# Five of the twelve products for xbc, in both layers of the first block, by seven part products instead of eight

## The chip, the cores and the metric

The kernel runs on one core of a Trainium2 chip, as one program and one launch. The metric is the device time in microseconds (us). The kernel before took 3345.99 us, the median of three runs that lay between 3344.57 and 3346.96 us. Everything is in 32-bit floats.

## What is computed

256 tokens of width 1024 go through a first block of two layers and then a second block of two layers. The change is in the layers of the first block. Cut to what matters, such a layer is:

```
h = h + 0.5 * swiglu(rms_norm(h), ffn1)
u = rms_norm(h, mix_norm)
(z_s, xbc, dt_s, qkv, z_d, b_d, a_d, gate_s, gate_d) = split(u @ w_in)
xbc = silu(causal_depthwise_conv(xbc, conv_w, conv_b))       # 4 taps, 3072 channels
y_s = state space branch of xbc, dt, z_s;  y_d = delta rule branch of qkv, z_d, b, a
h = h + (sigmoid(gate_s) * (y_s @ w_s) + sigmoid(gate_d) * (y_d @ w_d)) @ w_out
h = h + 0.5 * swiglu(rms_norm(h), ffn2)
```

The 3072 features of xbc come out of a matrix of 1024 x 3072, and the convolution along the tokens, one filter of four taps for each feature, is taken of them.

## The kernel before

Activations lie with features on the 128 partitions and tokens along the free dimension: `xT` holds the normed input as 8 tiles of 128 features x 256 tokens. The weights are read once, in order, as chunks of 1 MB (128 partitions x 2048 floats, 16 tiles of 128 x 128). SyncE issues one DMA for each chunk into a ring of three places; a place is written again when the first matmul of the chunk after it has run (`w_used`).

**A product.** A chunk of xbc gives 256 features (two tiles), and there are 12 chunks, so 12 products (named 0 to 11 below). `product` runs 16 matmuls with 256 tokens each, 8 for each of the two tiles, into one PSUM bank. Every matmul of 32-bit floats shows in the trace as two records. All matmuls of the large products have the line L331.

**By seven.** Other products of the kernel (`ffn1`, `z_d`, `gate_s` and others) take their chunk as a matrix of 2 x 2 quarters (half of the inputs, tile of the outputs), and the tokens as two halves of 128. The 2 x 2 by 2 x 2 product of quarters is then made with seven products of quarters in place of eight, at the price of sums: `tokens_by_dve` (L898 to L903) makes four sums of token quarters once for a stage, `weights_by_dve` (L885 to L890) four sums of weight quarters for every chunk, each an operation on VectorE (DVE) of 128 x 512, and `join` (L917 to L931) adds the seven results up in five operations, after ScalarE (ACT) has copied one of them out of PSUM (`part_by_act`, L842). On TensorE (PE) such a chunk is 28 matmuls with 128 tokens each. The first eight of them need only the chunk itself; ahead of the ninth, `seven` waits for all four weight sums of its chunk (`sum_by_dve`). The results are spread over two PSUM banks, X and Y, and both are asked for ahead of the first matmul.

**Banks.** The large products share four PSUM banks in turn (`Jobs`, `bulk_jobs`). `open_bulk` makes PE wait until the job of four places before has been read by its reader, ACT or DVE. Which engine reads is in the list of jobs.

**The stage of xbc, in program order of each engine.** The order of each engine is written out by hand; no planner is at work, and every engine runs its own list strictly in order.

- PE (`first_pe`): product 0 from an input that is not yet scaled (`opening`), product 1, the small product for dt, b and a (L1682), then products 2 to 11. Behind each of the products 3 to 10 stand four transposes (`rows`, L1690), behind product 5 also the running sums and the transpose of beta (L1703 to L1710), behind product 7 a transpose of the running sums (L1715).
- DVE (`first_dve`): the norm (L783), the scaling of product 0 into `pad` (L857), then the small chain for dt, which waits for the small product (L1277 to L1313, in turns with ACT), then for n = 0 to 11 the convolution `conv(n)`: six operations (L1331), three taps for each of the two tiles. After `conv(n)` come `rows` for n from 3 to 10 (L1342, two operations), after n = 5 `running_sums` (L1350 to L1374) and a copy of beta (L1386), after n = 7 a cast (L1390).
- ACT (`first_act`): its steps of the small chain, a table load, and then for each n `conv_in(n)`: it copies the bank into one of the two places of the padded input `pad` (L1045), and makes the last tap with the bias from the bank (L1051, two operations, which free the bank). For n = 0 the last tap is made from `pad` (L1033). `conv_silu(n - 1)` (L1056) follows.

`pad` is two places of two tiles with three zeros ahead of the 256 tokens, so that the taps are shifted views. The convolution n reads place n % 2. After xbc come the products of z_s and qkv, beside the attention-like products of the state space branch, and then z_d and gate_s by seven.

Of the kernel before, what the change touches and what calls it, by code (L numbers as in the profile page):

```python
# [11 lines left out]
ACT = mybir.ActivationFunctionType  # L12
# [4 lines left out]
S = 256  # L17
# [5 lines left out]
KF = FF // P  # L23
# [115 lines left out]
class Sems:  # L139
# [90 lines left out]
    def clear(self):  # L230
# [5 lines left out]

PER1 = {"silu_ready": 2 * KF, "conv_done": 24, "features_ready": 12, "qkv_tanh": 12, "qkv_ready": 12, "z_tanh": 8, "gates_ready": 8, "base_solved": 1, "zd_gated": 4,
        "y_summed": 4, "small_by_dve": 4, "small_by_act": 5, "dt_ready": 1, "split_ready": 1,  # L240
        "scales_ready": 4, "decay_ready": 20, "mix_ready": 16, "y_gated": 16, "squares_ready": 16, "rnorm_ready": 13,
        "normed": 16, "eg_ready": 4, "masked_ready": 4, "merge_ready": 4, "o_gated": 4, "parts_ready": 12}
# [30 lines left out]
class Tensor:  # L273
# [144 lines left out]
            if k == KD - 1 and done[m]:  # L418
                ins.then_inc(sems.bulk_done, 1)

    def by_seven(self, L, name, n, sums, norm=None, by_token=False):

        e, sems = self.e, self.sems
        where = by_sums(self.xT, sums.tx)
        made = {"T1": 1, "T2": 2, "T3": 3, "T4": 4}

        def ready(what, g):
            if what in ("B11", "B21"):
                e.wait_ge(sems.x_ready, scaled(norm) + g + 1 + (GROUPS if what == "B21" else 0))
            elif g == 0 and what in made:  # L430
                e.wait_ge(sems.tx_by_dve, TOKENS_FROM[L, name] + made[what])

        for i in range(n):
            X, Y = self.open_bulk(L, name, (i, 0)), self.open_bulk(L, name, (i, 1))
            if norm is not None and i == 0:
                self.opening((X[:, 0:S], Y[:, 0:S]), (True, True), norm)
                continue
            new = norm is not None and i == 1
            self.seven(sums, FAST_FROM[L, name] + i, range(GROUPS), X, Y, lambda what, g: where[what](g), True, True,
                       ready if new else None, new, by_token)  # L440

# [69 lines left out]
ROWS_AT, CUM_AT, CUM_T_AT = 3, 5, 7  # L511
STEPS = 19
BESIDE = [("z_s", i) for i in range(1, 8)] + [("qkv", i) for i in range(12)]


def bulk_jobs():
    spec = []
    for L in range(DEPTH):
        spec += both(L, "ffn1", KF) + both(L, "down1", PAIRS)
        spec += many(L, "xbc", 1, "dve") + many(L, "xbc", 11, "act", 1) + many(L, "z_s", 8, "dve") + many(L, "qkv", 12, "act") + both(L, "z_d", 4) + both(L, "gate_s", 4)  # L520

        spec += many(L, "branch_s", 4, "dve") + many(L, "gate_d", 4, "act") + many(L, "branch_s", 4, "dve", 4)
        spec += many(L, "branch_d", 4, "dve") + many(L, "w_out", KD, "dve")
        spec += both(L, "ffn2", KF) + both(L, "down2", PAIRS)
    for L in range(DEPTH, 2 * DEPTH):
        spec += both(L, "c_in", 8) + both(L, "q", 4) + both(L, "k", 4) + both(L, "v", 8)
        spec += both(L, "g", 8) + both(L, "gates", 8)
        spec += many(L, "kx", 4, "act") + [((L, "vx", (0, t)), "act") for t in range(NT)]
        spec += many(L, "ret_out", 8, "dve") + [((L, "vx", (1, t)), "act") for t in range(NT)]
        spec += many(L, "conv_out", 4, "dve") + many(L, "mix_out", KD, "dve")  # L530
        spec += many(L, "qx", 1, "dve") + many(L, "qx", 3, "act", 1) + many(L, "xo_out", KD, "dve")
        spec += both(L, "up", KF) + both(L, "down", PAIRS)
    return spec
# [64 lines left out]
def multiply_fast(L, name, at, chunks, parts, tokens, state=[0, 0], opening=0):  # L598

    FAST_FROM[L, name] = len(FAST) - opening  # L600
    FAST.extend(range(at + opening, at + chunks))
    PARTS_FROM[L, name], state[0] = state[0] - opening, state[0] + parts - opening
    if tokens:
        TOKENS_FROM[L, name], state[1] = state[1], state[1] + 4


for _L in range(DEPTH):
    multiply_fast(_L, "ffn1", _L * CHUNKS1, KF, KF, True, opening=1)
    multiply_fast(_L, "down1", _L * CHUNKS1 + KF, KF // 2, PAIRS, False)
    multiply_fast(_L, "z_d", _L * CHUNKS1 + 65, 4, 4, True)  # L610
    multiply_fast(_L, "gate_s", _L * CHUNKS1 + 69, 4, 4, False)
    multiply_fast(_L, "ffn2", (_L + 1) * CHUNKS1 - 33, KF, KF, True, opening=1)
    multiply_fast(_L, "down2", (_L + 1) * CHUNKS1 - KF // 2, KF // 2, PAIRS, False)
# [40 lines left out]
class First:  # L654


    def __init__(self, arena, small):
# [24 lines left out]

        self.seven_x = Seven(arena, sums_at, sums_at + 4096, sums_at + 6144)
        assert sums_at + 6144 + 2 * (2 * S + P) <= self.at
        self.sq_s = take(4 * S).rearrange("p (t n) -> p t n", n=S)
        self.rn_s = take(4 * S).rearrange("p (t n) -> p t n", n=S)
        pairs = lambda: take(2 * BANK).rearrange("p (s t n) -> p s t n", s=2, t=2)
# [309 lines left out]
def first_act(a, m, m2, L, par):  # L997
# [28 lines left out]
    def conv_in(n):  # L1026
        name, i = CONV1[n]
        dst = m.xbc if name == "xbc" else m.qkv
        if n == 0:

            e.wait_ge(sems.bulk_read_dve, BULK.read(L, name, i))
            for t in range(2):
                ins = e.activation(dst[:, t, :], m.pad[:, 0, t, 3:3 + S], ACT.Identity, scale=col("xbc_w", 4 * t + 3),  # L1033
                                   bias=col("xbc_b", t))
            ins.then_inc(sems.opened, 1)
            return
# [210 lines left out]
def first_dve(v, m, m2, L, par, cst, ring, ones):  # L1247
# [23 lines left out]
    e.memset(m.pad[:, :, :, 0:3], 0.0).then_inc(sems.dve_step, 1)  # L1271
    seen.up("dve_step")
    pair_opened_by_dve(v, m, L, "xbc", m.pad[:, 0, :, 3:3 + S])
    e.wait_ge(sems.chain_done, CHAIN.filled(L, "small", 0))
    b = bk[CHAIN.bank(L, "small", 0)]
    t = lambda i: m.tmp[:, i]
# [39 lines left out]
    def conv(n):  # L1316
        name, i = CONV1[n]
        dst, w = (m.xbc, "xbc_w") if name == "xbc" else (m.qkv, "qkv_w")

        if n:  # L1320
            e.wait_ge(sems.bulk_read_act, BULK.read(L, name, i))
        else:
            e.wait_ge(sems.opened, L + 1)
        for tap in range(3):
            for kk in range(2):
                tile = 2 * i + kk
# [49 lines left out]


    for n in range(12):
        conv(n)
        if ROWS_AT <= n < ROWS_AT + 8:  # L1380
            rows(n - ROWS_AT)
        if n == CUM_AT:
            running_sums()
# [277 lines left out]
def first_pe(t, m, m2, L, par, cst):  # L1661
# [30 lines left out]
        ins.then_inc(sems.chain_done, 1)  # L1692

    for i in range(1, 12):
        if i > 1:
            t.product((L, "xbc", i), xT)
        if ROWS_AT <= i < ROWS_AT + 8:
            rows(i - ROWS_AT)
# [1057 lines left out]
```

## Time and profile before

| | |
|---|---|
| median of three runs | 3345.99 us |
| the profiled execution | 3346.01 us |
| its span, first to last instruction | 3344.2 us |
| what lies around the span | 1.8 us |
| PE busy | 3300.1 us, 99% of the span |
| DVE busy | 2097.1 us, 63% |
| ACT busy | 646.9 us, 19% |
| mean granted clock of TensorE | 0.997 of full |

The profiled execution is as long as the median of the runs, so terms read from its trace can be set against that median directly. The stage of xbc lies from about 225 to 323 us in the first layer, and again some 926 us later in the second.

### The profile page before, as it was taken

The numbers are of one execution on the slowest core, as the hardware profiler recorded it, in microseconds if no ns is written. First come the engines' busy times: TensorE is split into PE (matmuls) and PEld (weight loads), VectorE is DVE, ScalarE is ACT, GpSimd is POOL, SyncE is SP. The second block draws the span as 40 slices with busy tenths as digits, with TensorE's granted clock in tenths as the row PEclk, the third lists the DMA queues.
The fourth block names the chain that finished last, engine by engine and source line by source line (L and its number), as shares of the span: only waits on it lengthen the run. The fifth ranks groups of instructions, "written<-read, shape, count | busy, mean of one in ns | idle before, by whom it ended". The sixth has DMA issues, their size and how long they took to land.

```text
span 3344.2 us, 55619 instructions
## 1 busy us (share of the span) xinstructions
PE 3300.1 (99%) x23518; PEld 3077.6 (92%) x23518; DVE 2097.1 (63%) x4698; ACT 646.9 (19%) x1431; POOL 245.1 (7%) x320
## 2 busy tenths in 40 slices
PE   8999999999999999999999999999999999999998
PEld 8998888989999988899899999978899999878998
DVE  6645575346666455754376698872487798852685
ACT  1113233211111132332211101201211111211211
POOL 0200000100102000001001000210012000210031
PEclk9999999999999999999999999999999999999999
DMA  5443343244444433432444344344344444343443
GB/s 194 166 153 138 127 148 128 71 151 164 171 167 168 153 138 137 143 128 82 159 168 164 139 173 169 127 154 149 116 167 164 166 172 164 126 143 121 152 172 132
DMA packets 80776, 495.20 MB, mean 148 GB/s; under 512 B 16880, under 2 KB 20880, under 8 KB 21392
## 3 DMA queue, kind: packets, MB, share of 16 engines
q1 hardware_dynamic: 70896, 490.57, 41.6%
q8 instruction: 186, 3.05, 0.4%
q10 hardware_dynamic: 9632, 1.08, 0.2%
q14 instruction: 62, 0.51, 0.0%
HBM read 490.03 MB, written 1.59 MB: 147 GB/s over the span
## 4 chain that ended last, share of the span: by engine, by line
PE 92%; DVE 6%; ACT 1%; issue 1%; POOL 0%; DMA 0%; SPq 0%; DVEq 0%; ACTq 0%
PE bank L331 84%; PE bank L1841 1%; PE bank L1834 1%; PE bank L480 1%; PE bank L1770 1%; DVE arena L1331 1%; DVE arena L888 1%; DVE arena L886 1%; DVE arena L890 1%; PE bank L2466 0%; PE bank L2405 0%; PE bank L1746 0%; DVE arena L885 0%; PE bank L2449 0%; ACT arena L2085 0%
## 5 line engine op out<-in xcount | busy, mean ns | idle before, releaser
L331 PE MATMUL bank<-arena,ring 128*128 128x256 f32 (+1 forms) x6160 | 1054.0, 325 | 13.5 <-DMA ring<-w 10.4
L331 PEld LDWEIGHTS bank<-arena,ring 128*128 128x128 f32 x6160 | 942.2, 191 | 99.2 <-issue 24.4
L331 PE MATMUL bank<-xT,ring 128*128 128x128 f32 (+1 forms) x5696 | 933.1, 320 | 0.0
L331 PEld LDWEIGHTS bank<-xT,ring 128*128 128x128 f32 x5696 | 839.7, 191 | 61.8 <-issue 0.7
L331 PE MATMUL bank<-arena 128*128 128x128 f32 x7392 | 875.5, 275 | 2.4 <-DVE arena L890 2.3
L331 PEld LDWEIGHTS bank<-arena 128*128 128x128 f32 x7392 | 849.8, 192 | 3.2 <-DVE arena L890 3.2
L885 DVE TENSOR_TENSOR arena<-ring 128x512 f32<-128x512 f32 x286 | 197.4, 690 | 120.4 <-PE bank L331 108.9
L842 ACT ACTIVATE arena<-bank 128x128 f32<-128x128 f32 x244 | 67.7, 278 | 943.2 <-PE bank L331 938.0
L331 PE MATMUL bank<-xT,arena 128*128 128x128 f32 x1632 | 216.2, 275 | 1.3 <-DVE arena L890 1.1
L917 DVE TENSOR_TENSOR arena<-arena,bank 128x256 f32<-128x256 f32 x244 | 102.0, 418 | 168.5 <-ACT arena L842 168.0
L890 DVE TENSOR_TENSOR arena<-ring,arena 128x512 f32<-128x512 f32 x286 | 201.0, 703 | 9.9
L2138 DVE SCALAR_TENSOR_TENSOR arena<-arena,par 128x256 f32<-128x256 f32 x480 | 204.4, 498 | 0.0
L886 DVE TENSOR_TENSOR arena<-ring 128x512 f32<-128x512 f32 x286 | 202.6, 708 | 0.0
L888 DVE TENSOR_TENSOR arena<-arena,ring 128x512 f32<-128x512 f32 x286 | 202.4, 708 | 0.0
L1331 DVE SCALAR_TENSOR_TENSOR arena<-arena,par 128x256 f32<-128x256 f32 x288 | 117.9, 480 | 133.0 <-ACT arena L1051 128.5
L331 PEld LDWEIGHTS bank<-xT,arena 128*128 128x128 f32 x1632 | 198.6, 192 | 2.4 <-DVE arena L890 2.4
L921 DVE TENSOR_TENSOR arena<-arena,bank 128x128 f32<-128x128 f32 x244 | 69.9, 286 | 113.6 <-PE bank L331 113.3
L986 POOL TENSOR_TENSOR arena<-arena 128x128 f32<-128x128 f32 x66 | 39.0, 591 | 1281.9 <-DVE arena L942 776.2
L766 ACT ACTIVATE xT<-hT 128x256 f32<-128x256 f32 x112 | 45.4, 414 | 309.3 <-DVE hT L821 244.1
L928 DVE TENSOR_TENSOR arena<-arena,bank 128x256 f32<-128x256 f32 x244 | 101.4, 415 | 3.3
L821 DVE SCALAR_TENSOR_TENSOR hT<-bank,hT 128x256 f32<-128x256 f32 x48 | 20.4, 425 | 127.2 <-PE bank L331 127.2
L2332 POOL TENSOR_TENSOR arena<-arena 128x512 f32<-128x512 f32 (+1 forms) x14 | 47.4, 3385 | 703.5 <-ACT arena L2016 680.8
(283 smaller groups left out, 2394.7 us busy)
## 6 DMA issues: line engine op xcount, KB each, us to landing
ring<-w SPq DMA_DIRECT2D x462, 1024.0 KB, 4.8
hT<-hT_d SPq DMA_DIRECT2D x4, 256.0 KB, 3.7
arena<-memT_d SPq DMA_DIRECT2D x1, 1024.0 KB, 7.6
outT<-hT SPq DMA_DIRECT2D x4, 256.0 KB, 2.2
cst<-cst_d SPq DMA_DIRECT2D x1, 796.5 KB, 9.8
arena<-dmask_d SPq DMA_DIRECT2D x1, 768.0 KB, 10.1
par<-p SPq DMA_DIRECT2D x2, 216.0 KB, 5.0
par<-p SPq DMA_DIRECT2D x1, 376.5 KB, 5.4
```

Of the source, the lines that this page charges most:

```text
L331: ins = self.e.matmul(out, lhsT, rhs, start=start, stop=stop)
L842: e.activation(seven.part[:, i % 2], a.banks[BULK.bank(L, name, (i, 0))][:, 0:P], ACT.Copy).then_inc(sems.part_copied, 1)
L885: e.tensor_tensor(s[:, 0, :], w[:, 2, :], w[:, 3, :], ALU.add).then_inc(sems.sum_by_dve, 1)
L886: e.tensor_tensor(s[:, 2, :], w[:, 0, :], w[:, 2, :], ALU.subtract).then_inc(sems.sum_by_dve, 1)
L888: e.tensor_tensor(s[:, 1, :], s[:, 0, :], w[:, 0, :], ALU.subtract).then_inc(sems.sum_by_dve, 1)
L890: e.tensor_tensor(s[:, 3, :], w[:, 1, :], s[:, 1, :], ALU.subtract).then_inc(sems.sum_by_dve, 1)
L917: e.tensor_tensor(quarter[:, 0:2, 0, :], twice(a), X[:, 1:3, :], ALU.add).then_inc(sems.dve_step, 1)
L921: e.tensor_tensor(quarter[:, 0, 1, :], u, Y[:, 1, :], ALU.add).then_inc(sems.dve_step, 1)
L928: e.tensor_tensor(last, twice(w), Y[:, 0:2, :], ALU.add).then_inc(sems.dve_step, 1)
L1331: ins = stt(y, m.pad[:, n % 2, kk, tap:tap + S], col(w, 4 * tile + tap), y, ALU.mult, ALU.add)
L2138: ins = stt(y, x, w, y, ALU.mult, ALU.add)
L2332: e.tensor_tensor(x[:, 0:n, :], x[:, 0:n, :], x[:, n:2 * n, :], ALU.add).then_inc(sems.pool_step, 1)
```

## The change

Five of the twelve products, those with the numbers in `BY_SEVEN = (2, 3, 6, 7, 10)`, are made by seven, under the name `xbc_7`. PE runs 28 matmuls of 128 tokens for each in place of 16 of 256. Each takes two banks, both read by DVE. The token sums are made once, and the weight sums of product 2 with them, behind the scaling of product 0 and ahead of the small chain. The weight sums of 3, 6, 7 and 10 stand ahead of everything that DVE does for n = 2, 5, 6 and 9, thus behind `conv(1)`, `conv(4)`, `conv(5)` and `conv(8)` with their rows. `join` writes straight into `pad`, in place; ACT then makes the last tap of these products from `pad`, as it did for product 0, and its copy of the bank into `pad` goes. For these products `rows` on DVE stands between the join and the convolution. The weight sums use the place of z_d and gate_s, the token sums that of gate_d, all of which are written later.

```
-PER1 = {"silu_ready": 2 * KF, ...
+PER1 = {"opened": 6, "silu_ready": 2 * KF, ...
...
+BY_SEVEN = (2, 3, 6, 7, 10)
...
-        spec += many(L, "xbc", 1, "dve") + many(L, "xbc", 11, "act", 1) + many(L, "z_s", 8, "dve") + ...
+        for i in range(12):
+            spec += [((L, "xbc_7", (BY_SEVEN.index(i), b)), "dve") for b in range(2)] if i in BY_SEVEN else many(L, "xbc", 1, "act" if i else "dve", i)
+        spec += many(L, "z_s", 8, "dve") + ...
...
+    multiply_fast(_L, "xbc_7", _L * CHUNKS1 + 33, BY_SEVEN, len(BY_SEVEN), True)
...
+        self.seven_xbc = Seven(arena, 40 * S + 24 * S, 40 * S + 40 * S, sums_at + 4096)
+        self.seven_xbc.c = self.pad[:, :, :, 3:3 + S]
...
     # conv_in(n), on ACT
-        if n == 0:
-
-            e.wait_ge(sems.bulk_read_dve, BULK.read(L, name, i))
-            for t in range(2):
-                ins = e.activation(dst[:, t, :], m.pad[:, 0, t, 3:3 + S], ACT.Identity, scale=col("xbc_w", 4 * t + 3),
+        if n == 0 or name == "xbc" and i in BY_SEVEN:
+
+            if n:
+                nth = BY_SEVEN.index(i)
+                part_by_act(a, m.seven_xbc, L, "xbc_7", nth)
+                e.wait_ge(sems.bulk_read_dve, BULK.read(L, "xbc_7", (nth, 1)))
+            else:
+                e.wait_ge(sems.bulk_read_dve, BULK.read(L, name, i))
+            for kk in range(2):
+                t = 2 * n + kk
+                ins = e.activation(dst[:, t, :], m.pad[:, n % 2, kk, 3:3 + S], ACT.Identity, scale=col("xbc_w", 4 * t + 3),
                                    bias=col("xbc_b", t))
             ins.then_inc(sems.opened, 1)
...
     # first_dve
     pair_opened_by_dve(v, m, L, "xbc", m.pad[:, 0, :, 3:3 + S])
+    tokens_by_dve(v, m, m.seven_xbc, 3 * L + 1, TOKENS_FROM[L, "xbc_7"])
+    weights_by_dve(v, m.seven_xbc, ring, FAST_FROM[L, "xbc_7"])
     e.wait_ge(sems.chain_done, CHAIN.filled(L, "small", 0))
...
     # conv(n), on DVE
-        if n:
+        if n == 0 or name == "xbc" and i in BY_SEVEN:
+            e.wait_ge(sems.opened, upto(L, "opened", 2 + BY_SEVEN.index(i) if n else 1))
+        else:
             e.wait_ge(sems.bulk_read_act, BULK.read(L, name, i))
-        else:
-            e.wait_ge(sems.opened, L + 1)
...
     for n in range(12):
+        if n > 1 and n + 1 in BY_SEVEN:
+            weights_by_dve(v, m.seven_xbc, ring, FAST_FROM[L, "xbc_7"] + BY_SEVEN.index(n + 1))
+        if n in BY_SEVEN:
+            join(v, m.seven_xbc, L, "xbc_7", BY_SEVEN.index(n), in_place=True)
+            if ROWS_AT <= n < ROWS_AT + 8:
+                rows(n - ROWS_AT)
         conv(n)
-        if ROWS_AT <= n < ROWS_AT + 8:
+        if ROWS_AT <= n < ROWS_AT + 8 and n not in BY_SEVEN:
             rows(n - ROWS_AT)
...
     # first_pe
     for i in range(1, 12):
-        if i > 1:
+        if i in BY_SEVEN:
+            t.by_seven(L, "xbc_7", (BY_SEVEN.index(i),), m.seven_xbc, 3 * L + 1, opens=False)
+        elif i > 1:
             t.product((L, "xbc", i), xT)
```

The rest of the diff lets `by_seven` and `multiply_fast` take a list of numbers in place of a count, and lets `by_seven` begin without an opening product; with it, the first of the five runs its part products in the order of a stage's first (`new`).

## Rows read from the trace of the kernel before

**Rows 1.** Page, part 1: busy us of each engine (share), instructions.
```profile
PE 3300.1 (99%) x23518; PEld 3077.6 (92%) x23518; DVE 2097.1 (63%) x4698; ACT 646.9 (19%) x1431; POOL 245.1 (7%) x320
```
**Rows 2.** Page, part 4: chain that ended last, by engine.
```profile
PE 92%; DVE 6%; ACT 1%; issue 1%; POOL 0%; DMA 0%; SPq 0%; DVEq 0%; ACTq 0%
```
**Rows 3.** Waits of PE: who, for whom, us in total, times, longest.
```profile
PE bank L331 <- DVE arena L890: 3.3, 4, 1.1
```
**Rows 4.** Timeline of PE, xbc, first layer: start, us, instruction, records.
```profile
241.95 14.04 PE L331 MATMUL bank<-xT,ring 128*128 128x256 f32 x64
...
255.84 0.60 PE L1690 MATMUL bank<-cst,arena 128*128 128x128 f32 x4
256.27 7.07 PE L331 MATMUL bank<-xT,ring 128*128 128x256 f32 x32
263.18 0.60 PE L1690 MATMUL bank<-cst,arena 128*128 128x128 f32 x4
...
270.53 0.60 PE L1690 MATMUL bank<-cst,arena 128*128 128x128 f32 x4
...
272.11 7.07 PE L331 MATMUL bank<-xT,ring 128*128 128x256 f32 x32
```
**Rows 5.** Timeline of PE, products z_d by seven, first layer.
```profile
479.97 1.06 PE L331 MATMUL bank<-xT,arena 128*128 128x128 f32 x8
...
486.22 1.06 PE L331 MATMUL bank<-xT,arena 128*128 128x128 f32 x8
...
493.16 1.16 PE L331 MATMUL bank<-xT,arena 128*128 128x128 f32 x8 [0.53 <-DVE arena L890]
```
**Rows 6.** Timeline of DVE, xbc, first layer; brackets: idle before, releaser.
```profile
232.89 0.68 DVE L857 TENSOR_TENSOR arena<-bank,rstd 128x512 f32<-128x512 f32 x1
...
242.15 0.26 DVE L1277 TENSOR_TENSOR arena<-bank,par 128x96 f32<-128x96 f32 x1 [8.59 <-PE bank L1682]
...
248.33 7.21 DVE L1331 SCALAR_TENSOR_TENSOR arena<-arena,par 128x256 f32<-128x256 f32 x18 [2.23 <-ACT arena L1033]
...
272.27 2.47 DVE L1331 SCALAR_TENSOR_TENSOR arena<-arena,par 128x256 f32<-128x256 f32 x6 [4.21 <-ACT arena L1051]
...
277.21 0.27 DVE L1386 COPY small<-bank 16x128 f32<-16x128 f32 x1
```
**Rows 7.** Timeline of ACT, xbc, first layer.
```profile
247.20 1.09 ACT L1033 ACTIVATE arena<-arena,par 128x256 f32<-128x256 f32 x2
...
248.68 1.00 ACT L1051 ACTIVATE arena<-bank,par 128x256 f32<-128x256 f32 x2
```
**Rows 8.** Timeline of DVE, z_d: first and last weight sum, join, what follows.
```profile
490.49 0.69 DVE L885 TENSOR_TENSOR arena<-ring 128x512 f32<-128x512 f32 x1
...
492.42 0.69 DVE L890 TENSOR_TENSOR arena<-ring,arena 128x512 f32<-128x512 f32 x1
493.02 0.41 DVE L917 TENSOR_TENSOR arena<-arena,bank 128x256 f32<-128x256 f32 x1
...
494.40 0.76 DVE L1480 SCALAR_TENSOR_TENSOR arena<-arena 128x256 f32<-128x256 f32 x2
```
**Rows 9.** Page, part 6: DMA of a chunk, KB, us to landing.
```profile
ring<-w SPq DMA_DIRECT2D x462, 1024.0 KB, 4.8
```
**Rows 10.** Timeline of PE, where the first block hands over to the second.
```profile
1873.13 1.13 PE L480 MATMUL bank<-xT,ones 128*128 128x256 f32 x4 [1.38 <-ACT xT L766]
1877.40 3.75 PE L331 MATMUL bank<-arena,ring 128*128 128x256 f32 x8 [3.15 <-ACT arena L770]
```
**Rows 11.** Windows of 1 us: busy by engine, granted clock (PEclk), DMA share, GB/s.
```profile
1875.00:1876.00 1.00, 0.00 (x0) 0.00 (x0) 0.84 (x3) 0.98 (x2) 0.00 (x0) 0.79 0.00 0
...
1882.00:1883.00 1.00, 1.00 (x6) 0.83 (x5) 0.00 (x0) 0.20 (x1) 0.00 (x0) 0.80 0.69 287
...
3087.00:3088.00 1.00, 0.95 (x6) 0.69 (x6) 0.42 (x2) 0.83 (x2) 0.00 (x0) 0.65 0.00 0
...
3090.00:3091.00 1.00, 1.00 (x4) 0.79 (x4) 0.00 (x0) 0.00 (x0) 0.00 (x0) 0.64 0.00 0
```

More of the change, by code:

```diff
@@ L235, in clear @@
         self.nc.all_engine_barrier()
-PER1 = {"silu_ready": 2 * KF, "conv_done": 24, "features_ready": 12, "qkv_tanh": 12, "qkv_ready": 12, "z_tanh": 8, "gates_ready": 8, "base_solved": 1, "zd_gated": 4,
+PER1 = {"opened": 6, "silu_ready": 2 * KF, "conv_done": 24, "features_ready": 12, "qkv_tanh": 12, "qkv_ready": 12, "z_tanh": 8, "gates_ready": 8, "base_solved": 1, "zd_gated": 4,
         "y_summed": 4, "small_by_dve": 4, "small_by_act": 5, "dt_ready": 1, "split_ready": 1,
@@ L419, in opening, with by_seven @@
                 ins.then_inc(sems.bulk_done, 1)
-    def by_seven(self, L, name, n, sums, norm=None, by_token=False):
+    def by_seven(self, L, name, n, sums, norm=None, by_token=False, opens=True):
         e, sems = self.e, self.sems
@@ L431, in ready @@
                 e.wait_ge(sems.tx_by_dve, TOKENS_FROM[L, name] + made[what])
-        for i in range(n):
+        for i in range(n) if isinstance(n, int) else n:
             X, Y = self.open_bulk(L, name, (i, 0)), self.open_bulk(L, name, (i, 1))
-            if norm is not None and i == 0:
+            if opens and norm is not None and i == 0:
                 self.opening((X[:, 0:S], Y[:, 0:S]), (True, True), norm)
                 continue
-            new = norm is not None and i == 1
+            new = norm is not None and i == opens
             self.seven(sums, FAST_FROM[L, name] + i, range(GROUPS), X, Y, lambda what, g: where[what](g), True, True,
@@ L519, in bulk_jobs @@
         spec += both(L, "ffn1", KF) + both(L, "down1", PAIRS)
-        spec += many(L, "xbc", 1, "dve") + many(L, "xbc", 11, "act", 1) + many(L, "z_s", 8, "dve") + many(L, "qkv", 12, "act") + both(L, "z_d", 4) + both(L, "gate_s", 4)
+        for i in range(12):
+            spec += [((L, "xbc_7", (BY_SEVEN.index(i), b)), "dve") for b in range(2)] if i in BY_SEVEN else many(L, "xbc", 1, "act" if i else "dve", i)
+        spec += many(L, "z_s", 8, "dve") + many(L, "qkv", 12, "act") + both(L, "z_d", 4) + both(L, "gate_s", 4)
         spec += many(L, "branch_s", 4, "dve") + many(L, "gate_d", 4, "act") + many(L, "branch_s", 4, "dve", 4)
@@ L600, in multiply_fast @@
     FAST_FROM[L, name] = len(FAST) - opening
-    FAST.extend(range(at + opening, at + chunks))
+    FAST.extend(range(at + opening, at + chunks) if isinstance(chunks, int) else [at + i for i in chunks])
     PARTS_FROM[L, name], state[0] = state[0] - opening, state[0] + parts - opening
@@ L1028, in conv_in @@
         dst = m.xbc if name == "xbc" else m.qkv
-        if n == 0:
-            e.wait_ge(sems.bulk_read_dve, BULK.read(L, name, i))
-            for t in range(2):
-                ins = e.activation(dst[:, t, :], m.pad[:, 0, t, 3:3 + S], ACT.Identity, scale=col("xbc_w", 4 * t + 3),
+        if n == 0 or name == "xbc" and i in BY_SEVEN:
[8 more added lines that the diff above has]
+                ins = e.activation(dst[:, t, :], m.pad[:, n % 2, kk, 3:3 + S], ACT.Identity, scale=col("xbc_w", 4 * t + 3),
                                    bias=col("xbc_b", t))
             ins.then_inc(sems.opened, 1)
+            seen.up("opened")
             return
```

## The prediction

> **What bounds the kernel now.** I read the page's busy times first: PE is busy for 99% of the span, DVE for 63%, ACT for 19% [rows 1]. The chain of waits agrees, it runs over PE for 92% [rows 2]. So a microsecond that PE saves counts, but any microsecond that PE is made to wait counts too, and there is almost nothing of that kind now: the list of PE's waits has 3.3 us, in four waits, for the weight sums of products by seven [rows 3], and none at all in the stage of xbc. Next I took PE's timeline of this stage, to price a product [rows 4], and of z_d, to price one by seven [rows 5]; then DVE and ACT in the same stretch, since the change gives DVE new work in a fixed order [rows 6, 7]. The second layer repeats these rows; every figure for one layer counts twice.
>
> **What PE saves.** A plain product is 32 records in 263.18 - 256.27 = 6.91 us [rows 4]. One by seven, start to start, takes 486.22 - 479.97 = 6.25 us for 56 records, 0.112 us each [rows 5]. That is 0.66 us for a product, 3.3 us for five, and 6.6 us for both layers if nothing else happened.
>
> **Product 2.** It starts at 241.95 [rows 4]. DVE is free at 232.89 + 0.68 = 233.57. The weight sums take 490.49 to 493.11, 2.62 us [rows 8]; the token sums are four operations of the same shape, so I take 2.7 for them too. They end at 238.9, inside the idle time of 8.59 us ahead of 242.15 [rows 6], so the small chain is not delayed and PE finds its sums there. Product 2 ends at 248.20, 0.66 earlier than a plain one.
>
> **Product 3 is where the gain goes.** Two waits come up here.
> First, it asks for two banks at once. The second is the one of product 1, and ACT frees that at 248.68 + 1.00 = 249.68 [rows 7], behind its part of the small chain. PE waits from 248.20 to about 249.75, 1.55 us. A plain product 3 asked for one bank only and never met this.
> Second, PE then does the eight matmuls that need the chunk alone, 16 records, 1.79 us, to 251.54, and waits for the weight sums of its own chunk. DVE does them ahead of n = 2, thus behind conv(0) and conv(1). These start at 248.33, because ACT gives the last tap of product 0 only then (the 2.23 us of idle in front of them are not used by the new sums), and are 12 of 18 operations that take 7.21 us, a pitch of 0.40: they let the next operation start at 253.1 [rows 6]. Plus 2.62 [rows 8] makes 255.7. In the trace PE starts 0.05 us after the last sum (492.42 + 0.69 = 493.11, and 493.16 in rows 5). So PE stands still from 251.54 to 255.75, 4.2 us. Behind these sums on DVE's queue stand the join of 2, which frees the banks of products 4 and 5, and conv(2), which the transposes behind product 5 need. The join is over 1.4 us later [rows 8], at 257.2, before PE comes to product 4, so nothing on PE waits for them.
> The other 40 records take 4.46, with 0.1 more for the first (1.16 against 1.06, rows 5): product 3 ends at 260.3. Before it ended at 255.84, less the latency some 255.77 [rows 4]. PE is 4.55 us late.
> Bounds for the two waits together: 0 if DVE's order did not matter (a wait can't save time, so not below), and 5.75 + 1.4 if a join (494.40 - 493.02, rows 8) came in front of the sums too. I take 5.75, the sum above, since all its rows are from this very stretch.
>
> **Products 6, 7 and 10.** DVE idles 4.21 us ahead of a convolution [rows 6], and 2.62 us of sums go in there: 6 and 10 are covered. 7 is the tight one. Its sums follow conv(5), its rows, the running sums and the copy of beta: 272.27 to 277.48, 5.21 us [rows 6]. The convolution starts 272.27 - 270.46 = 1.81 us behind the product (270.53 less 0.07). Sums ready: 1.81 + 5.21 + 2.62 + 0.05 = 9.7 us behind the end of product 5. PE needs them after the transposes and running sums, 272.11 - 270.53 + 0.07 = 1.65, the whole of product 6, 6.25, the rows, 0.43, and 1.79: 10.1. So 0.4 us are left. If that cover goes, it costs what is missing, some tenths. The joins, 1.4 us each [rows 8], and the last tap from `pad`, 1.09 [rows 7], lie in DVE's remaining idle time; ACT loses a copy for each. Banks: product 7's second is freed by ACT 1.8 us behind product 5, long before. Three times 0.66 gives back 1.98 us.
>
> **DMA.** A chunk lands 4.8 us after its issue [rows 9] and is issued two chunks ahead, so 6.25 us a chunk is fast enough, as it is in z_d. Nothing, below and above.
>
> **Sum without the clock.** 4.55 - 1.98 = +2.57 us a layer, +5.1 for both.
>
> **The clock.** Between 1873.13 - 1.38 = 1871.75 and 1877.40 PE worked 1.13 us, with pauses of 1.38 and 3.15 [rows 10]. The granted clock fell from full (2.4 GHz) to half (1.2 GHz) late in the microsecond 1875 (mean 0.79) and came back in the one that starts at 1882 (mean 0.80) [rows 11]. There 8 records took 3.75 us where 32 take 7.07 at full clock [rows 4, 10], twice as long each. So PE worked at half clock from 1877.4 to 1882.4, 5.0 us, and lost 2.5. At 3087 it fell after a thin stretch of the same sort and came back 3.4 us later, all of it under work [rows 11]: 1.7 lost. In our case PE works 1.79 us between 248.20 and 255.75 and pauses 1.55 and 4.2, a share of 0.24, against 0.20 in the first stretch (1.13 of 5.65) and one unbroken pause longer than any there. I expect a fall in each layer, at a cost between 0 and 2.5, and take 1.7: work resumes as densely as in the second case. +3.4 us for both layers.
> The Trainium skill (TensorE: Matmul & The Clock Gate, "Why this matters for your kernels") tells one to leave no idle gaps between bursts of matmuls if throughput is not to drop in mid-kernel. The trace agrees, with the half clock of rows 11 behind the pauses of rows 10. By this rule the sum is +8.5; without it, it is +5.1.
>
> **Total.** The profiled execution took 3346.01 us, span 3344.2 and 1.8 around it, and the median is 3345.99, so nothing is to be scaled. 3346.0 + 5.1 + 3.4 = 3354.5 us. What this measurement can tell from no change is about 0.2%, 6.7 us; the forecast of +8.5 lies above it.
>
> **Rivals.**
> *The clock stays up, in one layer or in both.* For it: the fall depends on when a pause falls, and the small waits in z_d (rows 3, up to 1.1) left no mark. Against: rows 10 and 11. Time: 3351.1 with none, 3352.8 with one; within 0.2%.
> *More waits.* The sums of 7 come later than my 0.4 us of room, or the late join holds a bank. It would add 0.5 to 2 us a layer: 3355.5 to 3358.5. For it: DVE's queue is in order and these stages stand close. Against: the sum for 7 closes, and the banks are free by several microseconds.
> *The other side: PE finds the sums of 3 ready, and the whole saving is kept.* It decides at 249.99, when the eighth matmul of product 3 ends if it starts at 248.20. It takes a DVE that does these sums ahead of conv(0), or in the 2.23 us of idle in front of it. Then, with the bank wait gone as well, -6.6: 3339.4; with the bank wait left, -3.3 + 1.55 = -1.75 a layer: 3342.5. For it: 2.23 of the needed 2.62 us are idle there. Against: the order of DVE's list puts conv(0) and conv(1) first.
> *Lateness is absorbed.* If PE's waits further on (L890 in z_d, rows 3) hang on chains that do not move with it, part of 2.57 us is lost in them. The largest is 1.1, so 3352 to 3354; I fold it into the range.
>
> **Chances.** Forecast with the clock down in both layers 0.66; clock up in one or both 0.17; more waits 0.07; the other side 0.10 (some of it for what I have not seen at all). The likeliest time is 3354.5. Its own range is 3352 to 3356.5, from clock costs of 1.0 to 2.5 a layer. The range for 8 in 10 goes from 3350.5, below the case without a fall, to 3357.5. Slower by over 0.2% has 0.62 of the forecast's case, less its low end, and the 0.07: 0.67. Within 0.2%: 0.26. Faster: 0.07.
>
> **What the profile of the changed kernel would show.** Right, if PE's waits have two new entries for a layer in this stage: one of about 4.2 us for the last weight sum (L890's successor), one of about 1.5 for ACT's last tap of product 1, and if product 3 ends near 260.3 (or later by the clock); if products by seven take 6.25 there; if the first product of z_s starts 2.6 us later than before in the first layer, or 4.3 with the clock. A clock under 1.00 in the windows between 254 and 261 us shows the third term. Wrong, if PE passes product 3 without a pause, if a wait shows at product 7, or if the small chain on DVE begins later than 242.15.

## The result, and the profile after

The changed kernel takes 3355.75 us, the median of nine runs (3354.79 to 3358.35), against 3346.96 for the kernel before in nine runs beside it (3344.48 to 3347.67). The ratio is 1.0029 with a 95% interval of 1.0021 to 1.0037: slower by 8.8 us. The profiled execution took 3358.35 us, span 3356.6, and is the longest of the nine.

The page of the changed kernel, parts 1 and 4, answers to [rows 1, 2]:

```profile
PE 3300.0 (98%) x23758; PEld 3086.8 (92%) x23758; DVE 2142.5 (64%) x4796; ACT 644.3 (19%) x1431; POOL 244.6 (7%) x320
...
PE 91%; DVE 6%; ACT 1%; issue 1%; POOL 0%; DMA 0%; SPq 0%; DVEq 0%; ACTq 0%
```

PE is as busy as before (3300.0 against 3300.1 us) although ten products should have freed it of 6.6 us, and the span is 12.4 us longer. So about as much was lost in slower matmuls as was saved, and the span grew by waiting.

PE's waits over the whole run (who, for whom, us in total, times, longest) answer to [rows 3], whose L890 is now L900:

```profile
PE bank L331 <- DMA ring<-w: 12.3, 1, 12.3
PE bank L331 <- DVE arena L900: 11.2, 6, 4.0
...
PE bank L331 <- issue: 2.7, 2, 1.4
```

The four waits of the kernel before are still there, 3.3 us in all: two of 0.5 in z_d, and two of 1.1 in the second block. Two of 3.95 have joined them, one in each layer. "issue" is the wait for the bank of product 1: the view names no releaser for it, and e4 and e5 below show what it hangs on. The three rows account for the span: 1.9 + 7.9 + 2.7 = 12.5 us more waiting than before. The first row is the first chunk's transfer at the start of the run, where nothing was changed. PE waited 10.4 us there in the profiled execution before and between 10.5 and 11.5 in those of the experiments, so the 1.9 us are put down to variation between executions, and are left out of what follows.

PE's timeline of xbc in the first layer (start, us, instruction, records, idle before and its releaser) answers to [rows 4, 5]:

```profile
244.01 2.02 PE L331 MATMUL bank<-xT,ring 128*128 128x128 f32 x16
245.87 1.06 PE L331 MATMUL bank<-xT,arena 128*128 128x128 f32 x8
246.76 2.84 PE L331 MATMUL bank<-arena 128*128 128x128 f32 x24
249.44 1.06 PE L331 MATMUL bank<-arena,ring 128*128 128x128 f32 x8
251.85 2.02 PE L331 MATMUL bank<-xT,ring 128*128 128x128 f32 x16 [1.35 <-issue]
257.83 2.08 PE L331 MATMUL bank<-xT,arena 128*128 128x128 f32 x8 [3.95 <-DVE arena L900]
259.70 4.52 PE L331 MATMUL bank<-arena 128*128 128x128 f32 x24
264.06 1.06 PE L331 MATMUL bank<-arena,ring 128*128 128x128 f32 x8
264.95 0.60 PE L1715 MATMUL bank<-cst,arena 128*128 128x128 f32 x4
...
287.91 1.95 PE L331 MATMUL bank<-xT,ring 128*128 128x128 f32 x16
289.70 1.06 PE L331 MATMUL bank<-xT,arena 128*128 128x128 f32 x8
...
316.20 13.98 PE L331 MATMUL bank<-xT,ring 128*128 128x256 f32 x64
```

The first four lines are product 2, without a wait. The next four are product 3, with both waits in it. Behind the second one the same operation is twice as long: eight records in 2.08 us where product 2 has 1.06, 24 in 4.52 where it has 2.84. The last line is product 11.

DVE's timeline, same kernel and layer, answers to [rows 6, 8]:

```profile
240.12 0.69 DVE L900 TENSOR_TENSOR arena<-ring,arena 128x512 f32<-128x512 f32 x1
244.21 0.26 DVE L1296 TENSOR_TENSOR arena<-bank,par 128x96 f32<-128x96 f32 x1 [3.41 <-PE bank L1707]
...
250.40 4.84 DVE L1350 SCALAR_TENSOR_TENSOR arena<-arena,par 128x256 f32<-128x256 f32 x12 [2.23 <-ACT arena L1049]
255.16 0.68 DVE L895 TENSOR_TENSOR arena<-ring 128x512 f32<-128x512 f32 x1
...
257.08 0.69 DVE L900 TENSOR_TENSOR arena<-ring,arena 128x512 f32<-128x512 f32 x1
...
288.44 0.69 DVE L900 TENSOR_TENSOR arena<-ring,arena 128x512 f32<-128x512 f32 x1
```

ACT's timeline has the last tap of product 1, which frees the bank, and answers to [rows 7]:

```profile
250.75 1.00 ACT L1068 ACTIVATE arena<-bank,par 128x256 f32<-128x256 f32 x2
```

The sums for product 2 still leave 3.41 us of idle ahead of the small chain (L1296). Those for product 3 stand behind twelve operations of the convolutions 0 and 1 and end at 257.77; PE goes on at 257.83. Those for product 7 end at 289.13, and PE uses them at 289.70.

The windows (busy of each engine, granted clock, DMA share, GB/s) answer to [rows 11]:

```profile
256.00:257.00 1.00, 0.00 (x0) 0.00 (x0) 1.00 (x2) 0.00 (x0) 0.00 (x0) 0.70 0.43 180
257.00:258.00 1.00, 0.17 (x1) 0.18 (x2) 0.96 (x3) 0.00 (x0) 0.00 (x0) 0.50 0.00 0
...
262.00:263.00 1.00, 1.00 (x7) 1.00 (x6) 0.97 (x3) 0.00 (x0) 0.00 (x0) 0.50 0.00 0
263.00:264.00 1.00, 1.00 (x10) 1.00 (x10) 0.34 (x1) 0.28 (x1) 0.00 (x0) 0.89 0.00 0
```

The clock fell from 2.4 to 1.2 GHz at about 256.4, with PE idle since 253.9, and came back at about 263.2 (a mean of 0.89 is 0.22 us at half and 0.78 at full). PE thus worked 5.4 us at half clock. In the second layer it fell in the microsecond 1188 (mean 0.62, so at 1188.2) and came back at the start of 1195 (0.97): 5.9 us of work, from 1189.2.

**One measure for the stage.** From the start of product 2 to the start of product 11 in the first layer is 309.05 - 241.95 = 67.10 us before and 316.20 - 244.01 = 72.19 after: 5.09 longer. In the second layer the stretch from product 2 to product 8 is 51.01 against 45.06, 5.95 longer; product 10's 0.66 comes off that, so 5.3 for the whole. The two stages explain 10.4 of the 12.4 us of the spans, the first chunk 1.9. Everywhere else PE's instructions keep their distance from those of the kernel before to within some 0.1 us.

### The profile page after: what moved, and what is told of

Its sections match the earlier page's. It is cut to its first block, busy times and chain, and to the rows that moved or that the text cites. A ratio compares the mean times of both kernels' runs of the same rounds, so it can differ in the third digit from the quotient of the medians.

```text
span 3356.6 us, 56215 instructions
## 1 busy us (share of the span) xinstructions
PE 3300.0 (98%) x23758; PEld 3086.8 (92%) x23758; DVE 2142.5 (64%) x4796; ACT 644.3 (19%) x1431; POOL 244.6 (7%) x320
## 3 DMA queue, kind: packets, MB, share of 16 engines
HBM read 490.03 MB, written 1.59 MB: 146 GB/s over the span
## 4 chain that ended last, share of the span: by engine, by line
PE 91%; DVE 6%; ACT 1%; issue 1%; POOL 0%; DMA 0%; SPq 0%; DVEq 0%; ACTq 0%
PE bank L331 83%; DVE arena L1350 1%; PE bank L1868 1%; PE bank L1861 1%; PE bank L480 1%; PE bank L1797 1%; DVE arena L898 1%; DVE arena L896 1%; DVE arena L900 1%; PE bank L2493 0%; DVE arena L895 0%; PE bank L2432 0%; PE bank L1773 0%; PE bank L2476 0%; ACT arena L2112 0%
## 5 line engine op out<-in xcount | busy, mean ns | idle before, releaser
L331 PE MATMUL bank<-arena,ring 128*128 128x128 f32 (+1 forms) x6240 | 1064.7, 325 | 15.5 <-DMA ring<-w 12.3
L331 PEld LDWEIGHTS bank<-arena,ring 128*128 128x128 f32 x6240 | 952.7, 192 | 100.5 <-issue 26.3
L331 PE MATMUL bank<-arena 128*128 128x128 f32 x7632 | 907.6, 276 | 2.4 <-DVE arena L900 2.3
L331 PE MATMUL bank<-xT,ring 128*128 128x128 f32 (+1 forms) x5536 | 882.5, 315 | 2.7 <-issue 2.7
L331 PEld LDWEIGHTS bank<-arena 128*128 128x128 f32 x7632 | 881.3, 193 | 3.1 <-DVE arena L900 3.1
L331 PEld LDWEIGHTS bank<-xT,ring 128*128 128x128 f32 x5536 | 798.7, 191 | 56.5 <-issue 3.7
L895 DVE TENSOR_TENSOR arena<-ring 128x512 f32<-128x512 f32 x296 | 204.0, 689 | 122.3 <-PE bank L331 105.2
L331 PE MATMUL bank<-xT,arena 128*128 128x128 f32 x1712 | 228.9, 277 | 9.1 <-DVE arena L900 9.0
L331 PEld LDWEIGHTS bank<-xT,arena 128*128 128x128 f32 x1712 | 210.0, 193 | 10.7 <-DVE arena L900 10.7
L927 DVE TENSOR_TENSOR arena<-arena,bank 128x256 f32<-128x256 f32 x254 | 106.2, 418 | 170.9 <-ACT arena L852 170.4
L900 DVE TENSOR_TENSOR arena<-ring,arena 128x512 f32<-128x512 f32 x296 | 207.9, 702 | 10.3
L896 DVE TENSOR_TENSOR arena<-ring 128x512 f32<-128x512 f32 x296 | 209.1, 707 | 0.0
L938 DVE TENSOR_TENSOR arena<-arena,bank 128x256 f32<-128x256 f32 x254 | 105.5, 415 | 4.4
```

The lines of the kernel that those rows point to most:

```text
L331: ins = self.e.matmul(out, lhsT, rhs, start=start, stop=stop)
L895: e.tensor_tensor(s[:, 0, :], w[:, 2, :], w[:, 3, :], ALU.add).then_inc(sems.sum_by_dve, 1)
L896: e.tensor_tensor(s[:, 2, :], w[:, 0, :], w[:, 2, :], ALU.subtract).then_inc(sems.sum_by_dve, 1)
L900: e.tensor_tensor(s[:, 3, :], w[:, 1, :], s[:, 1, :], ALU.subtract).then_inc(sems.sum_by_dve, 1)
L927: e.tensor_tensor(quarter[:, 0:2, 0, :], twice(a), X[:, 1:3, :], ALU.add).then_inc(sems.dve_step, 1)
L938: e.tensor_tensor(last, twice(w), Y[:, 0:2, :], ALU.add).then_inc(sems.dve_step, 1)
```

## Experiments

Each is an edit of the changed kernel. "The stage" is the stretch just defined, in the first layer. The first four shared one set of runs of the kernel before (3346.19 us), e5 to e7 another (3346.29), e8 a third (3346.1).

### e1: the weight sums of product 3 ahead of the convolutions

```
+    weights_by_dve(v, m.seven_xbc, ring, FAST_FROM[L, "xbc_7"] + BY_SEVEN.index(3))
     for n in range(12):
-        if n > 1 and n + 1 in BY_SEVEN:
+        if n > 2 and n + 1 in BY_SEVEN:
```

> The weight sums of product 3 stand ahead of conv(0) on DVE, not behind conv(1). My theory (PE waits for these sums, and the pause lowers the clock): the sums end about 248.7 us, before PE asks for them, conv(0) starts some 0.4 us later, and the wait of 4 us goes with the fall of the clock in both layers; only the wait for the bank of product 1, 1.4 us a layer, is left. Five products save 3.3 us a layer, so about 3343.5 us, 3.5 under the kernel before. Rival A (the place of these sums does not matter, DVE as a whole is late): 3353 to 3356. Rival B (a pause of 1.4 us is enough for the clock to fall): about 3347 to 3349.

Measured: 3341.97 us (3340.76 to 3343.31), ratio 0.9989 with 0.998 to 0.9998. This is 4.2 us under its own runs of before, where 3.5 were expected, and far from the 3353 us of rival A. The stage takes 65.41 us, 1.69 under before, and the clock stays at full in it, so rival B is out too. PE's timeline of e1 around product 3, then DVE's:

```profile
249.51 2.02 PE L331 MATMUL bank<-xT,ring 128*128 128x128 f32 x16 [1.35 <-issue]
251.37 1.06 PE L331 MATMUL bank<-xT,arena 128*128 128x128 f32 x8
```

```profile
245.73 0.69 DVE L895 TENSOR_TENSOR arena<-ring 128x512 f32<-128x512 f32 x1
...
247.66 0.69 DVE L900 TENSOR_TENSOR arena<-ring,arena 128x512 f32<-128x512 f32 x1
248.27 4.83 DVE L1350 SCALAR_TENSOR_TENSOR arena<-arena,par 128x256 f32<-128x256 f32 x12
```

The sums fill the idle time of DVE ahead of the convolution almost exactly: the convolution starts 6.60 us behind the start of product 2 (248.27 - 241.67), where it was 6.39 (250.40 - 244.01). The wait of 3.95 us is gone, and the bank wait is what remains. The place of one call is worth 13.8 us of the median (3355.75 less 3341.97; beside their own runs of before, +8.8 against -4.2, it is 13.0).

### e2: product 3 as a plain product

```
-BY_SEVEN = (2, 3, 6, 7, 10)
+BY_SEVEN = (2, 6, 7, 10)
```

(and the count of `opened`, and the place in `pad` of the join taken from n, as in e6 and e8)

> Only the products 2, 6, 7 and 10 are made by seven, 3 is plain again. My theory: neither of the two waits of product 3 comes up, the clock stays at full in this stage, four products save 0.66 us in each layer: 3347 - 5.3 = 3341.7 us. Rival (products by seven are as such too dear in this stage, through DVE's load or the banks, whichever products they are): at or above 3346 us.

Measured: 3340.47 us (3338.82 to 3344.25), ratio 0.9985 with 0.9977 to 0.9994. Beside its own runs of before it is 5.7 us faster, where 5.3 were expected. The stage takes 64.48, 2.62 under before: four times 0.66. The plain product 3 in e2's timeline of PE starts without a wait:

```profile
249.14 7.07 PE L331 MATMUL bank<-xT,ring 128*128 128x256 f32 x32
```

So the other four products gain what they should, and the whole loss belongs to product 3, both waits included.

### e3: unused matmuls inside the wait

```
         product(X, 1, lambda g: a(1, g), "B21", False, False)
+        for j in range(fill):      # 9 in product 3, 0 elsewhere
+            self.mm(Y[:, 0:S], self.whole[:, j * P:(j + 1) * P], self.xT[:, j % KD, :], True, True)
         e.wait_ge(sems.sum_by_dve, 4 * f + 4)
```

Nothing uses their results, which the next matmul into Y overwrites.

> As the changed kernel, but PE runs nine more matmuls of 128 x 256 (3.9 us at full clock) ahead of its wait for the weight sums of product 3, into a bank that the product overwrites afterwards; their results are used by nobody. They lie in time in which PE stood still, so they cost nothing by themselves. My theory (the fall of the clock costs 1.7 to 2.9 us a layer beside the wait): the granted clock stays at full, and the time is 3.4 to 5.8 us under the changed kernel's 3355.75, thus 3350 to 3352.4. Rival (the wait alone is the loss and the clock costs nothing): 3355.5, or later if the added matmuls run beyond the wait.

Measured: the stage takes 69.63 us, 2.56 less than after and 2.53 over before. This is the predicted sum without the clock, 2.57. The whole time, however, is 3353.95 us (3349.31 to 3355.2), ratio 1.0022 with 1.0013 to 1.0031, above the 3350 to 3352.4 that were expected, and only 1.8 us under the changed kernel. The expectation held for the stage and failed for the whole. e3's timeline of PE has product 3 and, further down, the second block:

```profile
250.70 5.91 PE L331 MATMUL bank<-xT,ring 128*128 128x128 f32 x34 [1.35 <-issue]
256.67 1.16 PE L331 MATMUL bank<-xT,arena 128*128 128x128 f32 x8
...
2264.62 0.70 PE L2424 MATMUL bank<-arena,cst 128*128 128x256 f32 x2 [2.03 <-POOL arena L2366]
2265.16 8.73 PE L331 MATMUL bank<-ring,arena 128*128 128x512 f32 x16
```

and its windows:

```profile
256.00:257.00 1.00, 0.94 (x6) 0.52 (x5) 0.97 (x3) 0.00 (x0) 0.00 (x0) 1.00 0.00 0
...
2265.00:2266.00 1.00, 1.00 (x4) 0.64 (x3) 0.00 (x0) 0.61 (x2) 0.00 (x0) 0.80 0.00 0
2266.00:2267.00 1.00, 1.00 (x2) 0.34 (x1) 0.78 (x2) 0.98 (x2) 0.00 (x0) 0.50 0.00 0
```

With work in the wait the clock holds in the stage, which shows that the half clock of product 3 comes from PE's idle time and not from the kind of its work. The same pause of 2.03 us that the kernel before has in its second block now ends in a half clock there, and again at 2992. The kernel before runs those 16 records in 7.03 us:

```profile
2259.49 0.70 PE L2394 MATMUL bank<-arena,cst 128*128 128x256 f32 x2 [2.03 <-POOL arena L2336]
2260.02 7.03 PE L331 MATMUL bank<-ring,arena 128*128 128x512 f32 x16
```

8.73 less 7.03 is 1.7 us, and 8.35 less 7.03 at the second place 1.3. Two smaller terms nearly cancel: the first chunk came 0.9 us later than in the profile before, and at the handover of [rows 10] the half clock lasted 3.4 us (1883.3 to 1886.7, from means of 0.65 and 0.64 in these two microseconds) instead of 6.8, which gives back 0.8. So the profiled span is 3344.2 + 2 x 2.53 + 3.0 + 0.9 - 0.8 = 3352.4, against 3352.5.

The unused matmuls are not what makes the clock fall there. e1 and e6 have none and show the same, e1 at the second pause and e6 at the first. e1's timeline and window:

```profile
2980.32 0.82 PE L2422 MATMUL bank<-arena,cst 128*128 128x256 f32 x2 [2.02 <-POOL arena L2364]
```

```profile
2981.00:2982.00 1.00, 1.00 (x3) 0.48 (x2) 0.00 (x0) 0.79 (x2) 0.00 (x0) 0.50 0.00 0
```

Why a pause that costs nothing in one kernel costs the clock in another is open.

### e4: the bank of product 1 freed early

ACT's `conv_in(1)`, which frees the bank, goes ahead of its part of the small chain. It then waits for DVE's reading of the bank of product 0, in place of the last step of the small chain.

```
+    conv_in(1)
     e.wait_ge(sems.small_by_dve, upto(L, "small_by_dve", 1))
...
     for n in range(12):
-        conv_in(n)
+        if n != 1:
+            conv_in(n)
```

> As the changed kernel, but ACT makes its part of product 1 ahead of its part of the small chain, so that the bank of product 1 is free at about 240 us. The wait for the weight sums stays. My theory (the two waits lie one behind the other, and only the last wait, for the sums, sets the end of product 3): the bank wait of 1.4 us goes and the wait for the sums grows by as much, 3355 to 3356 as the changed kernel, give or take a microsecond for the clock. Rival (each wait costs by itself): 2.7 us less, 3353.

Measured: 3356.27 us (3355.86 to 3356.45), ratio 1.0031 with 1.0019 to 1.0044, no gain, as expected. PE's timeline of e4:

```profile
248.81 1.95 PE L331 MATMUL bank<-xT,ring 128*128 128x128 f32 x16
256.30 2.08 PE L331 MATMUL bank<-xT,arena 128*128 128x128 f32 x8 [5.54 <-DVE arena L900]
```

The bank wait is gone and the wait for the sums is 5.54 us in place of 3.95. The two stood in series on PE, but only the later one, DVE's chain, set the end: PE goes on 13.81 us behind the start of product 2, where it was 13.82. The stage takes 71.93, 0.26 less than after, and this is clock and not wait: 4.9 us of work ran at half clock (256.3 to 261.2, the mean of the microsecond 261 being 0.92) in place of 5.4.

### e5: both waits taken away

ACT's `conv_in(0)` and `conv_in(1)` ahead of the small chain, and the edit of e1.

> Both waits taken away: the weight sums of product 3 ahead of conv(0) on DVE, and ACT's part of the products 0 and 1 ahead of its part of the small chain. My theory: PE has no wait left in the stage of xbc, and the stage is 5 x 0.66 = 3.3 us shorter than before in each layer: 3346.2 - 6.6 = 3339.6 us, some 2.7 under the run with the sums alone (3341.97, of which 1.4 us a layer were the wait for the bank). Rival (the bank wait was covered by something else, or another wait takes its place): 3341 to 3343.

Measured: 3339.81 us (3338.57 to 3341.86), ratio 0.9983 with 0.9974 to 0.9991. The stage takes 63.82, 3.28 under before: five times 0.66. PE has no wait in it, and the total for L900 is back at that of [rows 3]:

```profile
PE bank L331 <- DVE arena L900: 3.3, 4, 1.1
```

Beside e1 the bank wait is worth 65.41 - 63.82 = 1.59 us a layer once the sums are early. The stage gained 0.26 in e4, where they were late. The edits are not quite the same, since e5 moves `conv_in(0)` too.

### e6: seven products by seven

e5 with `BY_SEVEN = (2, 3, 5, 6, 8, 9, 11)`.

> The same, with seven products (2, 3, 5, 6, 8, 9 and 11) by seven instead of five. My theory (what counts is only whether a chunk's weight sums are done before PE's ninth matmul of it): DVE has 4.2 us idle behind a plain product and takes in two by seven for each of them, so nothing waits and the stage is 7 x 0.66 = 4.6 us a layer shorter than before: about 3337 us. Rival (DVE's load in this stage is then too high and its queue runs late, at product 6 behind the running sums first): a wait on weight sums comes back, above 3339 us, with another fall of the clock above 3342.

Measured: 3346.55 us (3341.79 to 3349.68), ratio 1.0 with 0.999 to 1.0009; the expectation failed. PE's timeline of e6, then DVE's:

```profile
267.22 1.16 PE L331 MATMUL bank<-xT,arena 128*128 128x128 f32 x8 [2.11 <-DVE arena L900]
```

```profile
262.17 2.46 DVE L1353 SCALAR_TENSOR_TENSOR arena<-arena,par 128x256 f32<-128x256 f32 x6 [0.49 <-ACT arena L1037]
264.55 0.68 DVE L895 TENSOR_TENSOR arena<-ring 128x512 f32<-128x512 f32 x1
...
266.47 0.69 DVE L900 TENSOR_TENSOR arena<-ring,arena 128x512 f32<-128x512 f32 x1
```

The sums of product 5 stand behind `conv(3)`, whose input comes from the join of 3 and ACT's last tap. DVE has not yet caught up at n = 3: joins and sums of 2 and 3 lie in the same few microseconds. PE waits 2.1 us in each layer. In the second layer the clock falls behind this wait as well, in the middle of product 5, where 24 records take 4.42 us instead of 2.84:

```profile
1196.53 1.25 PE L331 MATMUL bank<-xT,arena 128*128 128x128 f32 x8 [2.10 <-DVE arena L900]
1197.57 4.42 PE L331 MATMUL bank<-arena 128*128 128x128 f32 x24
```

This is what the rival named, at product 5 and not at 6. A new wait of 3.5 us shows in e6's list, in the first layer only:

```profile
PE bank L1844 <- DMA arena<-base_d: 3.5, 1, 3.5
```

Together the waits are 7.7 us, against a saving of 14 x 0.66 = 9.2. The clock also fell behind the new wait (0.68 in the microsecond 610) and in the second block (0.71 in 2262). The profiled span is 2.6 us over before. From the start of product 2 to that of product 11 the stage is 65.54 us in the first layer, 1.6 under before, and 67.16 in the second, 0.1 over; the two products 11 take off 1.3. The new wait and the half clock behind it add 5.2, the time ahead of the first stage 0.9, and the rest takes off 0.6. Whether the new wait belongs to the change is open, since it shows once in the two layers of one profile. Without its 5.2 us this execution, 3348.68, would still be some 6 us above the expected 3337.

### e7: no pause at all in product 3

e4 with the fill of e3, 12 matmuls instead of 9.

> As the changed kernel, with ACT's part of product 1 made early, so that the whole wait of product 3 is in one piece ahead of the weight sums, 5.5 us, and with twelve unused matmuls of 128 x 256 (5.2 us) in it: PE has hardly a pause left while product 3 ends when it did. My theory: the stage is 2.6 us a layer longer than before and the clock stays at full in it, as in the run with nine such matmuls, where the stage of the first layer took 69.63 us against 72.19 in the changed kernel. For the whole kernel that is +5.1, about 3351.3 us. That the run with nine came out at 3353.95 I put down to falls of the clock at pauses of 2 us much later, in the second block, which come and go from one execution to the next; if so, this one lies between 3350 and 3354.5 again. Rival (the unused matmuls themselves cost, outside the stage): the profile shows a longer stage, above 70 us.

Measured: the stage takes 69.62, as e3's 69.63. e7's timeline of PE:

```profile
248.83 7.13 PE L331 MATMUL bank<-xT,ring 128*128 128x128 f32 x40
256.31 1.16 PE L331 MATMUL bank<-xT,arena 128*128 128x128 f32 x8 [0.36 <-DVE arena L903]
...
260.88 0.60 PE L1720 MATMUL bank<-cst,arena 128*128 128x128 f32 x4
```

The whole time is 3353.8 us (3348.84 to 3355.3), ratio 1.0019 with 1.001 to 1.0027. The eleven runs fall into two groups, 3348.8 to 3350.1 and 3353.3 to 3355.3. The profiled execution, of the second group, has the half clock at the same two places of the second block as that of e3. That this parts the groups is likely by its size (3.0 us in e3, of some 4.5 between the groups), and the mean granted clock on record for each run agrees: 0.998 in all four of the faster group, 0.997 in all seven of the slower. It was not tested further, as only one execution was profiled. Beside e4 the fill gives back 71.93 - 69.62 = 2.31 us of the stage by the clock alone: in both kernels PE goes on at 256.3 (256.30 and 256.31), and the 40 records last until 263.17 in e4 and until 260.88 in e7.

### e8: a sixth product where DVE has room

e5 with `BY_SEVEN = (2, 3, 6, 7, 9, 10)`.

> The kernel with both waits taken away, with product 9 by seven as well: 2, 3, 6, 7, 9 and 10. In the run with seven of them PE waited 2.1 us for the sums of product 5, which stood behind the late conv(3); here no product follows two others by seven within three, except 9 and 10 behind the plain 8, and the sums of 9 should be ready at about 302.5 us, one before PE asks. My theory (only the readiness of the sums counts): no wait on sums in the stage, 6 x 0.66 = 4.0 us a layer shorter than before, 3346.3 - 7.9 = 3338.4 us. Rival (DVE's load shows once six are made by seven): a wait on sums of some tenths to 2 us a layer, 3339.5 to 3343.

Measured: 3337.7 us (3335.9 to 3339.01), ratio 0.9974 with 0.9964 to 0.9985. The stage takes 63.16, 0.66 less than e5's, and has no wait. This is the best of the kernels: 8.4 us under before, and so some 17 under the changed one, which was 8.8 over.

| kernel | median | against its before | stage, against before |
|---|---|---|---|
| after | 3355.75 | +8.8 | +5.09 |
| e4 bank early | 3356.27 | +10.1 | +4.83 |
| e3 filled | 3353.95 | +7.8 | +2.53 |
| e7 filled, no pause | 3353.8 | +7.5 | +2.52 |
| e1 sums early | 3341.97 | -4.2 | -1.69 |
| e2 without 3 | 3340.47 | -5.7 | -2.62 |
| e5 both early | 3339.81 | -6.5 | -3.28 |
| e8 six | 3337.7 | -8.4 | -3.94 |

## Why the prediction was right, point by point

**What PE saves.** 0.66 us a product was right: the stage of e2, e5 and e8 is shorter by 2.62, 3.28 and 3.94, which is four, five and six times 0.66 to within 0.02. Product 6 takes 287.47 - 281.22 = 6.25 us in the trace after, as predicted.

**Product 2.** Right: no wait on PE, and 3.41 us of idle left ahead of the small chain. One sign of being wrong was a small chain that begins later than 242.15, and it begins at 244.21. But product 2 starts 2.06 us later too (244.01 against 241.95), behind the late first chunk, so the chain has kept its place beside PE's work.

**Product 3, the bank.** Predicted 1.55 us, measured 1.35, and at the place named: ACT's last tap of product 1 ends at 250.75 + 1.00 in the trace after, and PE goes on at 251.85. The sign in the profile was named wrongly: I looked for ACT as releaser, and the list says "issue". e4 moves ACT's operation alone, e5 beside the edit of e1, and the wait is gone in both.

**Product 3, the sums.** Predicted 4.2 us, measured 3.95 in each layer. The order of DVE's list was the cause, as e1 shows by changing nothing else.
Without the clock I had PE at the end of product 3 at 260.3 - 241.95 = 18.35 us behind the start of product 2. In e7 it is 260.88 - 242.51 = 18.37, the clock at full. With 1.98 given back the sum was +2.57 a layer; e3 and e7 show +2.53 and +2.52.

**Products 6, 7 and 10.** Right, the tight one too: 0.4 us of room predicted for 7, 289.70 - 289.13 = 0.57 measured. e6 shows what lies beyond: another set of products, and DVE's queue is late by 2.1 us.

**The clock.** The mechanism was right and its size was off. I took 1.7 us a layer between bounds of 0 and 2.5. The profiled execution has 72.19 - 69.63 = 2.56 in the first layer and, over the stretch to product 8, 51.01 - 48.25 = 2.76 in the second, with e3 as the kernel without the fall; e4 against e7 has 2.31. I chose the second stretch of [rows 11], where 3.4 us ran at half clock, because work resumed densely. PE's pause ahead of that stretch, which ends at 3085.40 us, was 1.80 us long, less than half of the one at hand. In the event the half clock lasted as long as in the first stretch, 6.8 us in each layer (256.4 to 263.2, 1188.2 to 1195.1) and 6.8 there (1875.6 to 1882.4), although the work behind the pause was dense. It fell only 1.4 and 1.0 us ahead of the work, so that 5.4 and 5.9 us of work ran in it, against 5.0 there: a little above my upper bound. Over the medians the term comes out smaller: 8.8 less 5.1 is 3.7 us for both layers, against 3.4 predicted and 5.3 in the profile. The profiled execution is 2.6 us above the median and the longest of the nine, with the first chunk 1.9 us late. The mean granted clock differs between the runs too: 0.996 in the four of 3354.79 to 3354.95 us, 0.995 in the five of 3355.75 to 3358.35. So less time seems to have run at half clock in some executions. In e4, whose six runs lie within 0.6 us, the term is 10.1 less 5.1, 5.0 us. The close hit of the total thus owes something to luck: with 5.0 for the clock the sum would have been 3356.1.

**Rivals.** The clock that stays up is out: it fell in both layers of the profile, and the mean granted clock is 0.995 or 0.996 in all nine runs, against 0.997 or 0.998 in every run of the kernel before that lists it. More waits, not seen: PE has no wait in the stage but the two of product 3. Lateness that is absorbed, not seen: the four waits of [rows 3] are 3.3 us as before. The prediction puts them in z_d with up to 1.1 us; z_d has two of 0.5, and the two of 1.1 are in the second block. Nor are they all that PE waited before: the same list has 10.4 us for the first chunk and rows of 4.0, 3.6 and 3.1 us in other stages. The stage of xbc has none, and this is what the sum rests on. The other side was a matter of DVE's order, as I had put it, and its two times were 3342.5 with the bank wait left and 3339.4 without it; the kernels that make the order so, e1 and e5, took 3341.97 and 3339.81.

**The net.** 3354.5 was predicted, 3355.75 measured, within the likeliest case's own range of 3352 to 3356.5. The clock costs of 1.0 to 2.5 a layer that it names as its source give 3353.1 to 3356.1; the rest of the width is not accounted for. The chances for slower by over 0.2%, 0.62 and 0.07, add up to 0.69 and not to 0.67.

## What to carry to other kernels

An operation put into an in-order queue has two prices, its own time, which was covered everywhere in the changed kernel, and the place at which it stands. For each new wait, find what is queued ahead of the operation that ends it, and look for idle time in front of that: here 2.62 us of sums went where 2.23 us were idle, delayed the convolution by 0.2 us, and turned +8.8 us into -4.2.
A wait on TensorE of some 4 us costs more than its length where the clock falls with it, here another 2.3 to 2.8 us; price it from a stretch of the same trace. Here the longer of two stretches would have been nearer in the profile, though over the medians of the changed kernel the term was only 3.7 us for both layers.
Of two waits in series take away the one whose chain ends last first; the other alone is worth nothing as a wait (e4: 0.26 us, all of it clock; 1.59 us in e5, where the sums come early).

## What the runs showed of the hardware that was not expected

The kernel before passes two pauses of 2.0 us in its second block at full clock. In e3 and e7 the same pauses, with the same work around them, were followed by half clock, 8.73 us where 7.03 are usual. e1 shows it at the second pause and e6 at the first, without unused matmuls. These kernels differ from the one before there only in the moment at which the pause comes. The changed kernel, some 7 us later there than e3, has both pauses and kept its clock.
The Trainium skill (TensorE: Matmul & The Clock Gate, "Why this matters for your kernels") warns of idle gaps between bursts of matmuls, but only of longer ones than 2.03 us. The pauses of 3.95 us agree with it; those of 2.03 in e3, followed by a clock of 0.50, do not.
Half clock also lasted on under full load: in the changed kernel PE was busy without a break from 257.83 to 263.2 before the clock came back.
Unused matmuls in the wait of product 3 kept the clock, as e3 and e7 show with 1.00 throughout the stage. They are a means of measurement rather than a remedy here, since early sums take away the wait itself.
